# A hybrid attention block on one core: sliding-window items moved to chosen tiles of the FoX loop

## What is computed

```python
y_swa = _swa_branch(qa, ka, va, sinks[i]) * jax.nn.silu(za)     # 2 kv heads, window of two chunks + meta, ALiBi, sinks
log_f = jax.nn.log_sigmoid((ff + b_forget[i]).astype(jnp.float32))
y_fox = _fox_branch(qf, kf, vf, log_f) * jax.nn.silu(zf)        # causal over all tokens, decay from cumsum(log_f)
merged = (jax.nn.sigmoid(ga + b_gate[i, 0]) * (y_swa @ w_up_swa[i])
          + jax.nn.sigmoid(gf + b_gate[i, 1]) * (y_fox @ w_up_fox[i]))
h = h + _rmsnorm(merged @ w_out[i], g_post[i])
```

## Time and profile before

| | |
|---|---|
| median of three runs | 831.99 us |
| profiled execution, its span | 832.1 us, 830.3 us |
| TensorE busy | 799.4 us, 96% of the span |
| VectorE, ScalarE, GpSimd busy | 499.4, 315.3, 348.4 us |
| attention stage | 492 to 647 us of the span |

### The profile page before, as it was taken

The page is one execution under the profiler, slowest core; times in us unless marked ns, Lnnn a source line. Parts: engine busy times, 40 slices in busy tenths (PEclk is TensorE's granted clock), DMA queues, the critical chain, the costliest instruction groups (busy, mean ns, idle before and its releaser), DMA issues.

```text
span 830.3 us, 12914 instructions
## 1 busy us (share of the span) xinstructions
PE 799.4 (96%) x4514; PEld 646.3 (78%) x4514; DVE 499.4 (60%) x1060; ACT 315.3 (38%) x648; POOL 348.4 (42%) x292
## 2 busy tenths in 40 slices
PE   3999999999999999999999999999998999999997
PEld 3999999988878888788787865666674788878885
DVE  7944778446776867645646355777777844442222
ACT  6422241333334323333333326666777223222111
POOL 4412224454435444444344414656785344512221
PEclk9999999999999999999999999999999999999999
DMA  9342423469957346366363599999900475352221
GB/s 297 104 128 53 129 65 105 136 165 265 238 165 204 106 140 182 104 173 179 91 179 105 131 249 226 239 224 227 241 1 2 158 222 148 106 185 95 96 82 76
DMA packets 122712, 125.00 MB, mean 151 GB/s; under 512 B 30116, under 2 KB 92404, under 8 KB 122648
## 3 DMA queue, kind: packets, MB, share of 16 engines
q1 hardware_dynamic: 121208, 119.92, 54.1%
q10 hardware_dynamic: 1440, 4.26, 1.3%
HBM read 90.93 MB, written 34.92 MB: 152 GB/s over the span
## 4 chain that ended last, share of the span: by engine, by line
PE 80%; issue 6%; DVE 5%; POOL 5%; ACT 2%; DMA 1%; DVEq 0%; SPq 0%; POOLq 0%; ACTq 0%
PE PS L1877 20%; PE PS L1878 19%; PE PS L1879 19%; PE PS L2126 4%; PE PS L2127 4%; PE PS L2128 3%; POOL acc L1235 3%; PE PS L1984 2%; DVE t_val L1615 2%; PE PS L2049 1%; PE PS L2064 1%; PE PS L1899 1%; PE PS L2029 1%; POOL probs L1211 1%; ACT p_fox L1388 1%
## 5 line engine op out<-in xcount | busy, mean ns | idle before, releaser
L1166 POOL TENSOR_TENSOR ops<-s_sum,ops 128x512 fp32r<-128x512 f32 x64 | 87.5, 1377 | 111.2 <-ACT ops L1264 111.2
L1877 PE MATMUL PS<-t_hi,ops 128*128 128x512 f32 x256 | 101.1, 395 | 0.0
L1878 PE MATMUL PS<-t_lo,ops 128*128 128x512 f32 x256 | 99.8, 390 | 0.0
L1879 PE MATMUL PS<-t_hi,ops 128*128 128x512 f32 x256 | 99.8, 390 | 0.0
L1166 POOL TENSOR_TENSOR ops<-raw,ops 128x512 fp32r<-128x512 f32 x48 | 65.5, 1365 | 69.0 <-ACT ops L1264 68.8
L1187 POOL TENSOR_TENSOR w_plain<-raw,w_plain 128x1024 fp32r<-128x1024 f32 x10 | 28.0, 2800 | 84.4 <-ACT w_plain L1293 84.4
L1694 DVE TENSOR_TENSOR z_tmp<-u,PS 128x512 f32<-128x512 f32 x48 | 33.0, 687 | 49.1 <-PE PS L1879 28.2
L1235 POOL TENSOR_TENSOR acc<-acc,p_fox 128x400 f32<-128x400 f32 (+5 forms) x76 | 59.9, 808 | 5.0 <-ACT p_fox L1388 4.0
L1264 ACT ACTIVATE ops<-s_sum 128x512 fp32r<-128x512 f32 x64 | 39.6, 623 | 52.8 <-DVE s_sum L1496 41.8
L1388 ACT ACTIVATE p_fox<-PS,neg_c_col 128x512 f32<-128x512 f32 (+5 forms) x112 | 54.3, 536 | 13.7 <-PE PS L2035 9.1
L1879 PEld LDWEIGHTS PS<-t_hi,ops 128*128 128x128 f32 x256 | 48.1, 188 | 10.6
(11 more groups left out here) (206 smaller groups left out, 2182.9 us busy)
## 6 DMA issues: line engine op xcount, KB each, us to landing
raw<-in_w_in_dram SPq DMA_DIRECT2D x34, 512.0 KB, 5.2
q_dram<-stage_b SPq DMA_DIRECT2D x32, 256.0 KB, 3.0
g_dram<-stage_b SPq DMA_DIRECT2D x32, 256.0 KB, 2.1
tanh_g<-g_dram SPq DMA_DIRECT2D x16, 512.0 KB, 4.1
max_k<-k_dram SPq DMA_DIRECT2D x16, 260.0 KB, 5.5
max_c<-neg_c_dram SPq DMA_DIRECT2D x8, 520.0 KB, 6.4
x_all<-in_x_dram SPq DMA_DIRECT2D x8, 512.0 KB, 7.7
raw<-in_w_in_dram SPq DMA_DIRECT2D x16, 256.0 KB, 4.7
```

Source lines behind the costliest of these rows:

```text
L1166: nc.gpsimd.tensor_tensor(ops[:, i % OPS, 1], op_source(p, name), ops[:, i % OPS, 0].bitcast(F32), ALU.subtract).then_inc(op_ready, 1)
L1877: pe.matmul(dst, hi_w, hi, start=first, stop=False)
L1878: pe.matmul(dst, hi_w, lo, start=False, stop=False)
L1879: return pe.matmul(dst, lo_w, hi, start=False, stop=last)
```

## The change

`FIRST_SLOT` and the rule that spread the 32 items evenly over the tiles are replaced by a table, `ITEM_TILES`, with eight tiles for each pair; each pair's items now start in that pair. The finishing of a first half moves from 4 to 8 tiles after its end to 2 to 5 tiles after it. Three of the last pair's splits move one tile later.

```diff
-FIRST_SLOT = 2
-REC_UNITS = ((4, 5, 6, 7, 8), (2, 3, 4, 5, 5))
+ITEM_TILES = ((2, 3, 4, 9, 10, 11, 12, 13), (1, 2, 3, 9, 10, 11, 12, 13), (1, 2, 3, 9, 10, 11, 12, 13),
+              (0, 1, 2, 3, 4, 5, 6, 7))
+REC_UNITS = ((2, 3, 4, 5, 5), (2, 3, 4, 5, 5))
-    spread = len(units) - 8 - FIRST_SLOT
-        slot = u >= FIRST_SLOT and next_item < ITEMS and (u + 1 - FIRST_SLOT) * ITEMS // spread > next_item
+        slot = x in ITEM_TILES[j]
-            turn = {9: PAIRS + 2, 10: PAIRS - 1, 11: PAIRS, 12: PAIRS + 1}
+            turn = {9: PAIRS + 2, 11: PAIRS - 1, 12: PAIRS, 13: PAIRS + 1}
```

## The result

The changed kernel takes 841.94 us (median of 5 runs, 841.31 to 845.22) where the kernel before takes 832.27 (5 runs, 831.61 to 833.61): a ratio of 1.0118, with a 95% interval of 1.0101 to 1.0135. The forecast was 835.1 with a range of 828 to 840. The direction was right and the size was not: +9.7 us where +3.1 were forecast.

A forecast was written before the change was run, and what follows sets the result against it. TensorE, busy 96% of the span, was taken as the bound. Start +0.8, T9 to T13 of pairs 0 to 2 +0.5, last pair +1.8 and loads 0 made 3.1 us on 832.1, for a median of 835.1 us; range 828 to 840.

The forecast's parts named there:

- The walk: Start of pair 0: following the first items through the engines gave 3.3 us of waits for 1.66, +1.6, counted half, +0.8.
- The low clock: Behind the start of pair 0: 1.9 us lost at a granted clock of 0.56, taken to come again at the same cost.
- T9 to T13 of pairs 0 to 2: New waits of 1.3 us per pair, 3.9, against 3.4 us of old waits that go: net +0.5.
- rival B: Waits only change places, new ones at T10 to T12 and in the last pair as long as the old: 832 us, chance 0.26.
- The meeting of fin and items: T9 of pairs 0 to 2: the fin meets a row of five items on VectorE; TensorE waits 1.3 us a pair.
- rival E: Pair 2's three additions beside a `split_up` take 1.8 instead of 0.63 us by shared ports: 3.5 us on top, 838.7, chance 0.02.
- The last pair up to T13: VectorE 96% busy up to T8, engines waiting for each other: 3.7 us of waits in T1 to T6, plus 0.85 for a `p_t` copy.
- The circle of VectorE and ScalarE: Last pair, T1 to T6: six turns of 3.9 us where each engine waits for the other, 23.9 us in all.
- The end: The last sliding outputs' split waits for an item ending in T10, ahead of `p_fox`: 0.75 us of waiting, bound 2.5.
- Loads: Sliding queries of pair 1 land at 532.3, needed in T1 at about 533: cost 0, cover 0.7 us, up to 2 if earlier.
- Rival A: Items and fins no longer meet; the 3.4 us of waits in pairs 0 to 2 go: 828.7 us, chance 0.22.
- D: Last pair costs its upper bound, +4 not +1.8, TensorE also waits at the up projections' start: 838.5 us, chance 0.09.

The follow-up runs named there:

- e7: The changed kernel with one split of the last pair (y slot 6) moved from T9 to T10: 839.85 us, ratio 1.0080.
- e6: The kernel before with VectorE's two clears of KB moved from T4 to T8 of pair 0: 831.51 us, ratio 0.9980.
- e8: The changed kernel with the old finishing for the first half of pair 2 alone: 840.84 us, ratio 1.0090.
- e5: The changed kernel with VectorE's two clears of KB moved from T4 to T8 of pair 0: 841.03 us, ratio 1.0089.
- e4: The kernel before with only the new finishing of first halves (reciprocals and fin in T6 to T9): 834.38 us, ratio 1.0018.
- e10: The changed kernel with old finishing of first halves, pair 0's first three items back at T3, T4, T6, and clears of KB in T8: 835.45 us, ratio 1.0028.
- e3: The changed kernel with the old finishing of first halves in all pairs (reciprocals T8 to T11, fin T12): 837.04 us, ratio 1.0046.
- e11: As e10, with eight items a pair, but those of pairs 0 to 2 spread over their tiles: 834.68 us, ratio 1.0007.
- e0: The changed kernel run once more without an edit, for a second trace: 842.79 us in one run.
- e9: The changed kernel with five of six `split_up` in T0 to T4 of pair 2, the sixth in T8 of pair 3: 843.09 us, ratio 1.0115.
- e2: The changed kernel with the last pair's items as before; one more item starts in pair 1, two more in pair 2: 840.17 us, ratio 1.0071.

## Why the prediction was wrong

**The start (+0.8 forecast; +1.65 of idle time measured in T0 to T8).** The walk was right: 2.9 + 0.4 us of waits forecast, 2.75 + 0.56 measured, at the place and by the operand that it named, and +1.6 of idle time where 1.65 came. What failed was the halving, "each step of this walk is taken at its latest, so I count half". The walk's sum came out in the trace, so halving took away 0.8 us that were there. T9 to T13 of pair 0 add 0.75 us of idle time, with 0.35 and 0.28 of it at T12 and T13. Pair 0 is 2.7 us longer in the trace. Without low clock it takes 37.97 us in the change (e7). The kernel before has no such trace; with its clears moved (e6) pair 0 takes 34.95 us and has 0.57 less idle time, which makes 35.5: +2.5.

**The low clock ("to come again and to cost the same").** This was a mis-sized term, and it can't be sized from one trace. Behind the same 2.75 us at T5 the granted clock fell in the change (0.67 and 0.90), and did not in e7. Behind the same 1.3 us at the end it fell in e8, and did not in e5, whose end takes 186.97 us, 1.7 less than the change's. At the end it also fell in e4, with 0.81 us of idle time in T13, and in e10, with 0.99, and not in e3 and e11, with 0.98. In T5 to T8 of pair 0 it fell in nine of the ten traces with the clears in T4 and in none of the four with the clears in T8 (e5, e6, e10, e11). What the runs do give is a mean. One minus the granted clock of the span, times the span, averages 3.2 to 3.7 us in the three groups of the kernel before, 6.2 in the change, 4.2 in e3 and 2.3 in e6 (the clock is given to three digits, so each carries up to 0.4). Of the 9.7 us, then, some 2.7 are low clock, by this estimate, and about 7 are other time. That more waits bring more low clock is what this suggests; e8, with one wait fewer than the change and 7.9, doesn't fit, and why the clock falls in one execution and not in the next stays open.

**T9 to T13 of pairs 0 to 2 (+0.5).** The prediction took 3.9 us of new waits in pairs 0 to 2 for 3.4 old ones. Behind T8 of pair 0 the change has 5.26 us of idle time up to the end of pair 2, where there were 3.35: +1.9. The row of items behind T9 has 0.75, 0.75 and 1.60 us of it, 3.1 and not 3.9. The term that was missing is 0.95 and 0.94 us for `p_t` at T4 of pairs 1 and 2. The prediction let the old waits go since "in T4 the second half's fin has no new item"; the item of T1 is multiplied by the values there. In pair 1 this is rival B's picture: 1.70 us of idle time for 1.68, at other places. The wait for `p_t` looks like a milder form of pair 0's start, three items in a row; no run took it apart.

The meeting of fin and items was forecast at 1.3 us in each pair. In pairs 0 and 1 the new finishing costs nothing measurable: T9 to the next T0 take 14.10 us with the new finishing and 14.04 with the old (e0, e3). In pair 2 it costs 1.7, and some 1.0 of that go with the `split_up` (e9); the other 0.8 belong to the fin's place in T9 (e9 against e8). The Trainium skill (SBUF — State Buffer, "SBUF: two separate sides") has the rule that a VectorE instruction with two SBUF inputs waits in full for a GpSimd instruction that has the shared ports. The trace agrees: 1.57 and 1.49 us beside a `split_up`, 0.63 and 0.69 without. I had it as rival E with 0.02; its size was off because only two of the three additions were slowed, by 1.7 us together, and only 0.9 of that reached the fin. GpSimd's `split_up` is not the only thing that makes the meeting cost: e5 has none in pair 0, but VectorE's clears stand in T8, and T9 to the next T0 take 15.10 us instead of 14.10. The fin starts 4.4 us behind the start of T9 in pairs 0 and 1 of the change, 5.3 in pair 2 and 5.4 in pair 0 of e5. So in these traces 1.0 us is the price of a fin that comes 0.9 to 1.0 us late, by a `split_up` or by other work on VectorE.

**The last pair up to T13 (4.55 us of waiting forecast where there were 2.95, +1.6).** This mechanism did not cost what it was to cost. The circle of VectorE and ScalarE was forecast at 23.9 us for T1 to T6, and it took 22.9, with 2.85 us of idle TensorE instead of 3.7. VectorE was busy for 24.82 us in T0 to T8, not 28.6: 77% of their 32.40 us, and not 96% of TensorE's work. T0 to T13 grew by 4.75 us, but idle time in it went from 2.96 to 2.90, so none of that is waiting.

**The end (0.75 us of waiting forecast where there were 0.58, +0.17).** The trace has 1.92 us of idle time in T13, +1.3, within the bound of 2.5. The end is 3.5 us longer: these 1.3, some 1.7 of low clock, and 0.4 of idle time in the up and output projections. "The split of the last sliding outputs now waits for an item that ends in T10 and stands ahead of `p_fox` on ScalarE" names the right chain, but only its last link was priced. Ahead of that item's gate VectorE has the last reciprocal, the fin and the split's own second half, 4.5 us in a row. The new finishing is the part that must be there: the old one leaves 0.98 us of idle time in T13 (e3). With the split moved a tile later 0.78 are left (e7), and the new finishing in the old order has 0.81 (e4). But taking back the last pair's items alone does not clear it: 1.74 us of idle time and 189.69 us (e2), since the fin and a split still stand on VectorE ahead of the last addition, and the first of the three `p_fox` in question waits for that. The prediction costed the finishing, the items and the splits each by themselves, and put the fin in pairs 0 to 2 only.

**Loads (0).** Right for the change, whose stage came to pair 1 later, without a wait. The condition set beside it was right too: in kernels that come earlier (e6, e10) TensorE waits 1.4 to 1.5 us.

**The sum.** The forecast was 3.1 us of waiting. In the trace the same four places have 1.65, 1.9, -0.06 and 1.3: 4.8 us. What makes the rest of the 10.7 us had no term: 1.7 of low clock behind the stage, 2.1 of busy time, 0.4 of idle time in the last stage, and 1.6 ahead of the attention stage in that execution. So three steps failed: the start was halved without a reason (0.8 us), the waits of pairs 1 and 2 and of the end were missed (1.4 and 1.2 us), and the low clock was priced at no change. That the forecast wasn't further off owes something to luck: 1.6 of its 3.1 us were put on the last pair up to T13, which cost no waiting.

Rival A falls: the waits of the earlier trace rows did go, but longer ones came at other places. B holds in pair 1 and not in the total. D had the end on its list ("and TensorE also waits at the start of the up projections") with 838.5, but for a VectorE that can't catch up in the last pair, and it did. E, at 838.7, was nearest in number and too small as well.

## What to carry to other kernels

When a change packs work that two engines share, walk each engine's queue through every place where two moved parts meet, the last tiles above all, and keep the walk's full result: halving it for caution had no ground in the rows here. Where TensorE is the bound, a wait's price has a second part that one trace can't show, since the clock may or may not fall behind it; give it a range of its own, and read it from the means of many runs. An edit that takes a step off one crowded place is measured by the length of the stretch, since the total can hide it behind what the step costs where it went.

## What the runs showed of the hardware

- Gaps of 0.50 and 1.16 us were followed by a granted clock of 0.56 for 4 us, and a gap of 2.74 us in e7 by a full clock. The runs of e7 differ by 6 us (838.04 to 844.02, with granted clocks of 0.997 and 0.990), and there the difference goes with the clock. It does not in every kernel: e3 has 835.50 us at 0.996 and 840.19 at 0.995.
- Between executions of different kernels a stretch of the same order repeats within 0.05 us when the clock is full: from the start of T5 to that of T9 pair 1 takes 9.91 or 9.92 us in each of e0, e3, e5, e7, e8 and e9.
